# Delta rule on raw convolved keys: inverse key norms applied to rows and products instead of to the keys

## The reference, cut to what matters

```python
def _l2norm(x):
    xf = x.astype(jnp.float32)
    return xf * lax.rsqrt(jnp.sum(xf * xf, axis=-1, keepdims=True) + EPS)
...
    kb = k * beta[..., None]
    a_strict = jnp.where(strict, jnp.einsum("bhnid,bhnjd->bhnij", kb, k) * decay, 0.0)
    t_mat = lax.linalg.triangular_solve(eye + a_strict, ...)
    u = jnp.einsum("bhnij,bhnjd->bhnid", t_mat, v * beta[..., None])
    w = jnp.einsum("bhnij,bhnjd->bhnid", t_mat, kb * jnp.exp(gc)[..., None])
    qk = jnp.einsum("bhnid,bhnjd->bhnij", q, k) * decay
```

## Time and profile before

| what | value |
|---|---|
| median of 3 executions | 1774.19 us (1773.76 to 1775.34) |
| the profiled execution | 1776.97 us, span 1775.2 us |
| TensorE busy | 1709.0 us, 96% of the span |
| VectorE, ScalarE, GpSimd busy | 667.4, 424.8, 174.3 us |
| mean granted clock of TensorE | 0.985 of 2.4 GHz |
| HBM read | 534.42 MB |

### The profile page before, as it was taken

The page is one execution under the profiler, slowest core; times in us unless marked ns, Lnnn a source line. Parts: engine busy times, 40 slices in busy tenths (PEclk is TensorE's granted clock), DMA queues, the critical chain, the costliest instruction groups (busy, mean ns, idle before and its releaser), DMA issues.

```text
span 1775.2 us, 23815 instructions
## 1 busy us (share of the span) xinstructions
PE 1709.0 (96%) x10164; PEld 1116.0 (63%) x10164; DVE 667.4 (38%) x760; ACT 424.8 (24%) x462; POOL 174.3 (10%) x247
## 2 busy tenths in 40 slices
PE   8999999999999999999999999999999999999896
PEld 7998989988788888887444443344344433443342
DVE  5356777456644645543122220222022202220222
ACT  6344354225522433343000000000000000000002
POOL 5000043310240200000000000000000000000001
PEclk9999999999999999999999999999999999999998
DMA  8455535334533555649999999999999999999997
GB/s 258 154 167 167 167 125 184 127 117 138 166 119 118 152 189 183 220 168 381 399 427 428 427 428 427 430 428 429 428 428 429 428 430 427 430 427 430 428 425 284
DMA packets 95336, 537.60 MB, mean 303 GB/s; under 512 B 5836, under 2 KB 5900, under 8 KB 70044
## 3 DMA queue, kind: packets, MB, share of 16 engines
q1 hardware_dynamic: 94672, 535.85, 76.0%
q0 software_dynamic: 592, 0.69, 0.4%
HBM read 534.42 MB, written 2.10 MB: 302 GB/s over the span
## 4 chain that ended last, share of the span: by engine, by line
PE 74%; DMA 21%; DVE 2%; ACT 1%; issue 1%; SPq 0%; POOL 0%; DVEq 0%; ACTq 0%; POOLq 0%
DMA arena<-in_w 20%; PE psum L2138 14%; PE psum L2165 10%; PE psum L1628 9%; PE psum L1629 9%; PE psum L1630 9%; PE psum L2057 4%; PE psum L1647 3%; PE psum L1649 3%; PE psum L1648 3%; PE psum L2182 1%; PE psum L2183 1%; PE psum L2098 1%; PE psum L1880 1%; PE psum L1834 1%
## 5 line engine op out<-in xcount | busy, mean ns | idle before, releaser
L2138 PE MATMUL psum<-arena 128*64 128x512 f32 x2048 | 460.4, 606 | 38.0 <-DMA arena<-in_w 37.1
L2138 PEld LDWEIGHTS psum<-arena 128*64 128x64 f32 x2048 | 148.6, 139 | 338.9 <-issue 287.9
L1087 DVE TENSOR_TENSOR w_lo<-arena,w_hi 128x2048 fp32r<-128x2048 f32 x119 | 276.1, 2323 | 196.2 <-ACT w_hi L758 188.9
L758 ACT ACTIVATE w_hi<-arena 128x2048 fp32r<-128x2048 f32 x119 | 227.6, 1914 | 271.9 <-PE psum L1630 196.3
L1628 PE MATMUL psum<-w_hi,hT_hi 128*128 128x512 f32 x568 | 229.0, 403 | 0.2 <-DVE w_lo L1087 0.2
L1629 PE MATMUL psum<-w_lo,hT_hi 128*128 128x512 f32 x568 | 226.0, 398 | 0.0
L1630 PE MATMUL psum<-w_hi,hT_lo 128*128 128x512 f32 x568 | 225.9, 398 | 0.0
L2165 PE MATMUL psum<-arena 128*64 128x512 f32 x960 | 210.4, 594 | 2.8 <-DMA arena<-in_w 2.8
L2165 PEld LDWEIGHTS psum<-arena 128*64 128x64 f32 x960 | 67.2, 137 | 134.7 <-issue 125.6
L1647 PE MATMUL psum<-hT_hi,w_hi 128*128 128x256 f32 x512 | 147.1, 287 | 0.0
L1649 PE MATMUL psum<-hT_hi,w_lo 128*128 128x256 f32 x512 | 145.6, 284 | 0.0
(11 more groups left out here) (398 smaller groups left out, 1484.6 us busy)
## 6 DMA issues: line engine op xcount, KB each, us to landing
arena<-in_w SPq DMA_DIRECT2D x184, 2048.0 KB, 26.2
arena<-in_w_in SPq DMA_DIRECT2D x87, 1024.0 KB, 5.0
arena<-in_w_out SPq DMA_DIRECT2D x16, 1024.0 KB, 5.1
arena<-in_w SPq DMA_DIRECT2D x14, 1024.0 KB, 19.9
arena<-in_w_oa SPq DMA_DIRECT2D x8, 1024.0 KB, 5.0
arena<-in_w_ob SPq DMA_DIRECT2D x8, 1024.0 KB, 5.1
arena<-in_x SPq DMA_DIRECT2D x4, 1024.0 KB, 7.0
arena<-in_w SPq DMA_DIRECT2D x4, 512.0 KB, 15.6
```

What stands on the lines that cost most here:

```text
L758: nc.scalar.activation(w_hi[x % NSPLIT], ringA[:, x % RING_A, :], ACT.Copy).then_inc(sem("w_hi"), 1)
L1087: tt(w_lo[x % RING_A], ringA[:, x % RING_A, :], w_hi[x % NSPLIT].bitcast(F32), ALU.subtract)\
L2138: i = mm(bank(w)[e * CAP:(e + 1) * CAP, :], xeT[:, k, e * CAP:(e + 1) * CAP], src[e][:, (k % 8) * CB:(k % 8 + 1) * CB], start=(k == 0), st ...
```

## The change: what it does

The matrices A and PT are computed from the convolved keys as they are. The transposed back keys (`khT`) and the scaling of the keys in token layout are gone. The norms of the keys come from the token layout: ScalarE squares the PSUM pair of `ktok`, VectorE sums along the channels, GpSimd takes the power. The norm step `ssq` keeps the queries alone, 8 matmuls in place of 16, and stands behind `vtok`. The squared inverse norms `rk2` multiply the rows of the first-level blocks and of the whole matrix, and two small vectors (`begr`, `bvr`) carry the norms into the scaled keys and the values. The convolutions run in the order keys, queries, values. The fills move: `ktok`, `A` and `PT` have none behind them now; `vtok` has 1 chunk, `ssq` 2, `Y1` 2 (group 0) or 1 (group 1), `o` 4 or 2. The loops over the convolution take `CONV_ORDER = (1, 0, 2)` and count their semaphores by place; their calls of `sp_.before` name `ktok` in place of `ssq`. The diff, cut to its core:

```diff
 GLA_STEPS = (["rbc", "small", "cw", "smallT", "blrT", "gc", "gkT", "lv_eye"]
              + [f"lv{b}" for b in LEVELS] + ["kd", "bS", "bo0", "bo1", "obT0", "obT1"])
-GDN_STEPS = (["gcb", "ssq", "ktok", "vtok", "khT", "A", "PT", "Y1"]
+GDN_STEPS = (["gcb", "ktok", "A", "PT", "vtok", "ssq", "Y1"]
              + [f"{w}{b}" for b in LEVELS[1:] for w in ("Tt", "Y", "dU") if b > 2 or w != "Tt"]
              + ["u0", "wT", "S", "v1", "oi", "o", "oaT"])
 STEPS = GLA_STEPS + [f"{s}.{g}" for g in range(NG) for s in GDN_STEPS]
 
+CONV_ORDER = (1, 0, 2)
 FIRST_BLOCKS = 2
 SPAN_BLOCKS = [7, 4 + PRE, 1 + NC]
 SPANS = [
...
      "lv4": 2, "lv8": 1, "lv16": 2, "lv32": 1, "lv64": 2, "kd": 1, "bo1": 3},
 ] + [
     {f"{k}.0": v for k, v in
-     {"gcb": 9, "ssq": 2, "vtok": 1, "khT": 1, "PT": 1, "dU2": 1, "dU4": 1, "dU8": 1, "dU16": 1, "dU32": 1,
-      "dU64": 1, "Y1": 1, "o": 3}.items()},
+     {"gcb": 9, "vtok": 1, "ssq": 2, "dU2": 1, "dU4": 1, "dU8": 1, "dU16": 1, "dU32": 1,
+      "dU64": 1, "Y1": 2, "o": 4}.items()},
     {f"{k}.1": v for k, v in
-     {"gcb": 8, "ssq": 1, "vtok": 1, "khT": 1, "PT": 0, "dU2": 1, "dU4": 1, "dU8": 1, "dU16": 1, "dU32": 1,
+     {"gcb": 8, "vtok": 1, "ssq": 2, "dU2": 1, "dU4": 1, "dU8": 1, "dU16": 1, "dU32": 1,
       "dU64": 1, "Y1": 1, "o": 2}.items()},
 ]
 
...
+            if base == "ktok":
+                return "ktok", 2 * g + 2
+            if base == "A":
+                return "A", 2 * g + 1
...
+                wait(pool, ("ksum", g + 1))
+                nc.gpsimd.tensor_tensor(rqk[:, 8:16], ssqk[:, 8:16], pw[:, 8:16], ALU.pow).then_inc(sem("rqk"), 1)
+
                 wait(pool, ("expDT", g + 1))
                 nc.gpsimd.tensor_tensor(units(T_["DT"]), units(T_["DT"]),
                                         upT.unsqueeze(1).to_broadcast([P, GU, P]), ALU.mult)\
                     .then_inc(sem("DTm"), 1)
 
-                wait(pool, ("ssqk", g + 1))
-                nc.gpsimd.tensor_tensor(rqk, ssqk, pw, ALU.pow).then_inc(sem("rqk"), 1)
-
-                wait(pool, ("ktok", g + 1))
+                wait(pool, ("ktok", 2 * g + 2))
                 k4 = T_["zT0"][:, 0:1024].rearrange("p (h n t) -> p h n t", h=GH, n=NM)
-                nc.gpsimd.tensor_tensor(T_["kbg"].rearrange("p (h n t) -> p h n t", h=GH, n=NM), k4,
-                                        mh(beg)[:, :, g * GH:(g + 1) * GH].rearrange("p n h -> p h n")
-                                        .unsqueeze(3).to_broadcast([P, GH, NM, P]), ALU.mult)
                 nc.gpsimd.tensor_tensor(units(T_["kdec"], GH), k4[:, :, 0, :],
                                         mh(ekd)[:, 0, g * GH:(g + 1) * GH].unsqueeze(2).to_broadcast([P, GH, P]),
-                                        ALU.mult).then_inc(sem("k_scaled"), 1)
-
-                wait(pool, ("A", g + 1))
+                                        ALU.mult)
+
+                wait(pool, ("A", 2 * g + 2))
                 for i, b in list(enumerate(LEVELS))[1:-1]:
                     if i >= 2:
 
@@ -682,6 +687,13 @@
                     dst = T_["gB"] if i % 2 == 0 else T_["L1"]
                     diagonal_blocks(dst, mask[b]).then_inc(sem("L"), 1)
                     pool.wait_ge(sem("L"), 5 * g + i)
+                    if i == 1:
+                        nc.gpsimd.tensor_tensor(T_["kbg"].rearrange("p (h n t) -> p h n t", h=GH, n=NM), k4,
+                                                begr.rearrange("p (h n) -> p h n", h=GH)
+                                                .unsqueeze(3).to_broadcast([P, GH, NM, P]), ALU.mult)\
+                            .then_inc(sem("k_scaled"), 1)
+                wait(pool, ("ssqk", g + 1))
+                link(nc.gpsimd.tensor_tensor(rqk[:, 0:8], ssqk[:, 0:8], pw[:, 0:8], ALU.pow))
                 wait(pool, ("a_ms", g + 1))
...
-                for i in range(2):
-                    act.wait_ge(sem("silu"), 3 * g + i + 1)
-                    nc.scalar.activation(T_[f"zT{i}"][:, 0:1024], c[i], ACT.Square).then_inc(sem("sq"), 1)
-                result("khT" + s)
-                nc.scalar.activation(T_["zT1"][:, 0:1024], pair("khT" + s), ACT.Copy).then_inc(sem("khT"), 1)
+                result("ktok" + s)
+                nc.scalar.activation(T_["zT1"], pair("ktok" + s), ACT.Square).then_inc(sem("ktok"), 1)
+                act.wait_ge(sem("silu"), 3 * g + 2)
+                nc.scalar.activation(T_["zT0"], pair("ktok" + s), ACT.Copy).then_inc(sem("ktok"), 1)
+                wait(act, ("ksum", g + 1))
+                nc.scalar.activation(T_["zT1"], c[0], ACT.Square).then_inc(sem("sq"), 1)
...
-                result("ssq" + s)
-                ts(ssqk, pair("ssq" + s)[:, 0:16], 4 * EPS, None, ALU.add).then_inc(sem("ssqk"), 1)
-                wait(dve, ("rqk", g + 1))
-                result("ktok" + s)
-                tt(units(T_["zT0"][:, 0:1024]), units(pair("ktok" + s)),
-                   rqk[:, 8:16].unsqueeze(2).to_broadcast([P, GU, P]), ALU.mult).then_inc(sem("ktok"), 1)
-                result("vtok" + s)
-                tt(u4(T_["zT2"][:, 0:1024]), u4(pair("vtok" + s)), per_unit(bhalf), ALU.mult)\
-                    .then_inc(sem("vtok"), 1)
+                sp_.before("ktok" + s)
+                dve.wait_ge(sem("ktok"), 2 * g + 1)
+                link(nc.vector.reduce_sum(ssqk[:, 8:16], units(T_["zT1"]), axis=AX.X))
+                ts(ssqk[:, 8:16], ssqk[:, 8:16], 4 * EPS, None, ALU.add).then_inc(sem("ksum"), 1)
                 result("A" + s)
                 wait(dve, ("DA", g + 1))
                 dve.wait_ge(sem("D1"), g + 1)
                 for r in range(2):
-                    i = tt(units(T_["gB"][:, 0:512])[ROWS[r]], units(pair("A" + s))[ROWS[r], :, r * HP:(r + 1) * HP],
-                           units(T_["gB"][:, 0:512])[ROWS[r]], ALU.mult)
-                i.then_inc(sem("L_first"), 1)
+                    tt(units(T_["gB"][:, 0:512])[ROWS[r]], units(pair("A" + s))[ROWS[r], :, r * HP:(r + 1) * HP],
+                       units(T_["gB"][:, 0:512])[ROWS[r]], ALU.mult)
                 tt(T_["Dm"], pair("A" + s), T_["Dm"], ALU.mult).then_inc(sem("A"), 1)
+                wait(dve, ("rqk", g + 1))
+                link(tt(rk2, rqk[:, 8:16], rqk[:, 8:16], ALU.mult))
+
+                def of_group(t):
+                    return mh(t)[:, :, hs_g].rearrange("p n h -> p h n")
+
+                def by_unit(t):
+                    return t.rearrange("p (h n) -> p h n", h=GH)
+
+                dve.wait_ge(sem("A"), 2 * g + 1)
+                tt(units(T_["gB"][:, 0:512]), units(T_["gB"][:, 0:512]), rk2.unsqueeze(2).to_broadcast([P, GU, HP]),
+                   ALU.mult).then_inc(sem("L_first"), 1)
+                tt(by_unit(begr), of_group(beg), by_unit(rk2), ALU.mult)
+                tt(by_unit(bvr), of_group(bhalf), by_unit(rqk[:, 8:16]), ALU.mult)
+                tt(units(T_["Dm"]), units(T_["Dm"]), rk2.unsqueeze(2).to_broadcast([P, GU, P]), ALU.mult)\
+                    .then_inc(sem("A"), 1)
                 result("PT" + s)
                 wait(dve, ("DTm", g + 1))
                 tt(T_["DT"], pair("PT" + s), T_["DT"], ALU.mult).then_inc(sem("PT"), 1)
+                result("vtok" + s)
+                dve.wait_ge(sem("A"), 2 * g + 2)
+                tt(units(T_["zT2"]), units(pair("vtok" + s)), bvr.unsqueeze(2).to_broadcast([P, GU, P]), ALU.mult)\
+                    .then_inc(sem("vtok"), 1)
+                result("ssq" + s)
+                ts(ssqk[:, 0:8], pair("ssq" + s)[:, 0:8], 4 * EPS, None, ALU.add).then_inc(sem("ssqk"), 1)
 
...
+                pe.wait_ge(sem("silu"), 3 * g + 1)
+                lvl("ktok", lambda o, u, sl: tr(o[:, sl], c[1][:, sl], ident))
+                lvl("A", lambda o, u, sl: mm(o[:, sl], c[1][:, sl], c[1][:, sl], start=True, stop=True))
+                pe.wait_ge(sem("silu"), 3 * g + 2)
+                lvl("PT", lambda o, u, sl: mm(o[:, sl], c[1][:, sl], c[0][:, sl], start=True, stop=True))
+                pe.wait_ge(sem("silu"), 3 * g + 3)
+                lvl("vtok", lambda o, u, sl: tr(o[:, sl], c[2][:, sl], ident))
                 open_pair("ssq" + s)
-                pe.wait_ge(sem("sq"), 2 * g + 2)
+                pe.wait_ge(sem("sq"), g + 1)
                 o = pair("ssq" + s)
-                for j in range(2):
-                    for u in range(GU):
-                        i = mm(o[:, 8 * j + u:8 * j + u + 1], T_[f"zT{j}"][:, u * P:(u + 1) * P], ones[:, 0:1],
-                               start=True, stop=True)
+                for u in range(GU):
+                    i = mm(o[:, u:u + 1], T_["zT1"][:, u * P:(u + 1) * P], ones[:, 0:1], start=True, stop=True)
                 done("ssq" + s, i)
                 fill("ssq" + s)
-                lvl("ktok", lambda o, u, sl: tr(o[:, sl], c[1][:, sl], ident))
-                pe.wait_ge(sem("silu"), 3 * g + 3)
-                lvl("vtok", lambda o, u, sl: tr(o[:, sl], c[2][:, sl], ident))
```

(39 more changed lines are left out.)

## The result

The changed kernel takes 1787.14 us (median of 6 executions, 1784.76 to 1788.15), the kernel before in the same runs 1774.66 us (6 executions, 1773.52 to 1779.41). The ratio is 1.0065, with a 95% interval of 1.0053 to 1.0077: slower by 11.5 us. The prediction was 1776.7 us, with a range from 1769 to 1782 us; the measured time lies 5.1 us above that range.

What follows compares the result with a forecast made beforehand. TensorE's program order, clock and waits bound the changed stretch; the expert stage shifts with it. Group 0 +3.45 us and group 1 -0.9 make +2.5 on 1774.19: 1776.7 us, range 1769 to 1782.

Steps and rivals of the forecast that it cites:

- Edits at nothing: Part on side effects: added VectorE and GpSimd work stays covered and costs nothing, no DMA is added, one copy comes late.
- The moved chunk shifts one thing: Group 0, last level: ScalarE's gate block stands ahead of the `u0` copy, so `S` waits about 0.35 us.
- The wait ahead of `vtok`: TensorE idles while VectorE and ScalarE work up to `Dm`, counting 0.3 us before `PT`: 7.0 us in group 0, 7.3 in group 1.
- The clock after the wait: Behind the wait TensorE runs at half rate for a time, costing 2.1 us a group, bounds nothing and 5.1 us.
- the rival of a clock that stays up: TensorE's clock does not fall through the waits ahead of `vtok`: 1772.5 us, chance 0.10.
- The saving in group 0: Norm step to `Y2`: 2.8 us norm matmuls, 0.87 `khT`, 2.2 chunks no longer at low clock; 6.0 us less.
- L785 and `S`: Group 0: a ScalarE gate block makes the `u0` copy late and `S` waits for it, 0.35 us, bounds 0 and 1.24.
- Group 1: Second group's sum: wait 7.3 us plus clock 2.1 less savings 10.3, so -0.9 us.
- The split was in the chain: Chunk 47's split delays VectorE's read of `A`, lengthening the `vtok` wait; rival that it does not: 1762.1 us, chance 0.10.
- the third: Rival: the clock falls at the short norm step as well, in both groups: 1780.1 to 1783.5 us, chance 0.15.
- The expert stage did not absorb what came ahead of it: Rival: the expert stage absorbs the front's savings and waits, so nothing is seen: 1774.2 us, chance 0.03.
- the +3.1 us of group 0 up to `Y2`: Group 0 without the late copy: wait +7.0 us, clock +2.1, saving -6.0.

Runs made afterwards that it cites:

- run 1: Changed kernel, with VectorE calling for the splits due by `Y2` ahead of the solve's levels in group 0: 1780.72 us, ratio 1.0035 to the kernel before.
- run 2: Changed kernel, with one chunk moved from `Y1` to `o` in group 0: 1780.80 us, ratio 1.0033 to the kernel before.
- run 9: Kernel before, with one chunk moved from `o` to `Y1` in group 0, so two at `Y1`: 1779.87 us, ratio 1.0038 to the unedited kernel before.
- run 11: Changed kernel, with GpSimd's masking of the decays (L670) moved behind VectorE's read of `A`: 1784.96 us, measured once.
- run 3: Changed kernel, with VectorE reading `A` before it makes the open split: 1778.18 us, ratio 1.0023 to the kernel before.
- run 4: Changed kernel, with one chunk moved from `ssq` to behind `PT` in both groups: 1770.69 us, ratio 0.9975 to the kernel before.
- run 5: Changed kernel, with 32 unused matmuls on TensorE between `PT` and `vtok` in both groups: 1783.04 us, ratio 1.0048 to the kernel before.
- run 10: Changed kernel, with GpSimd's scaling of the keys for the state (`kdec`, L676) moved behind the first masked blocks: 1784.39 us, measured once.
- run 12: Kernel before, profiled once more with nothing changed: 1775.93 us, measured once.
- run 6: Kernel before, with the keys' norm matmuls left out, 8 one-column matmuls in place of 16: 1768.83 us, ratio 0.9962 to the unedited kernel before.
- run 7: Changed kernel, with a chunk moved behind `PT` and the splits due by `Y2` called for earlier: 1765.38 us, ratio 0.9949 to the kernel before.
- run 8: Changed kernel, with a chunk behind `PT`, earlier splits due by `Y2`, and `A` read before the split: 1761.86 us, ratio 0.9932 to the kernel before.

## Why the prediction was wrong

**The step that failed** is in "Edits at nothing": "The moved chunk shifts one thing", the late copy at `S`. It shifts two; the second was put at nothing without a reason. It is the lookahead of VectorE's splits. With two chunks at `Y1`, `sp_.before("Y1")` comes with end = 48 and last = 46 and follows the chunks up to 47, so the last low part made is that of chunk 49, the second at `Y1`. The next call in VectorE's program is the one for `dU2`, behind whose fill chunk 50 stands; and its splits come behind the read of `dU2`. In the kernel before, with one chunk at `Y1`, the same call reached `dU2`'s own chunk. ScalarE's program has a call in between, VectorE's has none. The price is 3.7 us of waiting and, as the clock falls there too, 2.3 us more: 6.0 us in the trace, 5.3 to 6.4 us in runs 1 and 2, +5.9 us in the mirror, run 9. The prediction had the rule at hand (it used it for chunk 47) and counted the splits at one step only.

**The wait ahead of `vtok`** was right in its place, its reason and its size: 0.3 + 7.3 us in group 0 where 7.0 were forecast, 0.6 + 6.5 us in group 1 where 7.3 were. In group 0 the chain was 1.0 us longer, since GpSimd held up the split (run 11), and TensorE's steps beside it 0.4 us longer; the chain's other terms are within 0.1 us each. Run 3 and run 4 show both sides: less chain, or more work over it.

**The clock after the wait** was forecast at 2.1 us a group. In the profile of the changed kernel it was 2.6 us in group 0 and 2.7 us in group 1, against the same steps at 1.00 in run 5. It varies as well: by the same difference it is 1.4 to 2.3 us a group in the profiles of runs 1, 2, 10 and 11, whose code is the same there. The Trainium skill's rule ("TensorE: Matmul & The Clock Gate", Part 1: The HAM clock gate), that half rate is the resting state, was the right one of the two weighed: in both groups the clock fell while TensorE waited, in run 5, with matmuls in that time, it stayed at 1.00, and the rival of a clock that stays up is out.

**The saving in group 0** (6.0 us) was right against the profiled execution, and the changed kernel has its parts: 1.68 us of norm step and no low clock there. But the profile it was taken from had a long stretch of low clock. Against an execution like run 12's the saving is smaller by 1.6 us, and against one like run 9's by 3.1 us (18.2, 16.6 and 15.1 us from the norm step to `ktok`). That fits with the medians being 12.5 us apart and the profiled spans 10.5 us.

**L785 and `S`** (0.35 us): 0.25 us. From `u0` to `S` TensorE takes 2.1 us, where it took 1.85 us before. **Group 1**: -0.2 us where -0.9 was forecast; the clock cost 0.6 us more than forecast there.

**The rivals.** The split was in the chain; its rival is out. The clock did not fall at the short norm step (1.00 from 322.4 to 330.0 us, and in group 1 behind 506.8 us), so the third did not come about, though in run 6, behind a wait of 1.5 us, the clock did fall there. The expert stage did not absorb what came ahead of it: run by run its start and the span moved together (+11.6 and +10.5 us, in run 7 -11.6 and -12.7, in run 8 -14.4 and -15.9). The result lies 5.1 us above the range because no case in it held a second new wait, which is worth 6.0 us.

**The sum put right**: the +3.1 us of group 0 up to `Y2` become +5.0 (0.6 us more idle time, 0.5 us more for the clock, the rest in steps and chunks that were a little longer than taken); L785 gives 0.25; behind `dU2` there are +6.0; group 1 gives -0.2: +11.05 us, against spans 10.5 us apart. What stays open is what decides between no low clock, 3.4 and 6.8 us behind one and the same code.

## What to carry to other kernels

Where engines prepare work ahead by a rule on program order, every change of a table of fills must be followed through that rule for each engine and each step up to the next call, not only for the step that one looks at. A wait is best shortened from both ends: taking the split out of the chain gave 9 us, putting a chunk over it 16.5 us, and at either a look at who is late next is due (GpSimd, in run 3). Steps taken off the critical engine take with them the chunks that stood behind them, and these were the time in which VectorE and ScalarE caught up: one chunk put back was worth 16.5 us.

## What the runs showed of the hardware

- A stretch at 1.2 GHz can follow a run of one-column matmuls, without any idle time, but not always and not for the same time: 6.8 us, 3.4 us and none in group 0, in three profiles of the same instructions (before, run 12, run 9). A single profile is a weak basis for what removing it will save.
- Behind a wait of 6.3 to 7.3 us TensorE went on at 1.2 GHz and lost 1.4 to 2.7 us; waits of up to 1.6 us there left the clock at 1.00 (runs 4 and 7), and so did matmuls without use in the time of the wait (run 5).
- A VectorE multiplication or split with both inputs in SBUF and a GpSimd multiplication beside it went one after the other: 2.29 us became 3.32, 0.69 became 2.87, and on GpSimd 1.03 became 3.08. GpSimd's power on 128×8 did not hold a split up (2.29 us beside it, group 1).
- GpSimd's power on 128×8 took 1.64 us, on 128×16 2.91 us.
